# Five units in the opening in place of three, sums kept in SBUF, softmax and last convolution group one pair sooner

## What is computed

```python
c_act = jax.nn.silu(c)
for i in range(DEPTH):                       # DEPTH = 2
    mod = c_act @ ada_w[i] + ada_b[i]        # 2048 x 12288
    sh_mix, sc_mix, g_mix, sh_mlp, sc_mlp, g_mlp = jnp.split(mod, N_MOD, axis=-1)
    h = modulate(rmsnorm(x, norm_mix[i]), sh_mix, sc_mix)   # h*(1+scale)+shift
    mix = fox_mixer(h, ...) if i % 2 == 0 else short_conv_mixer(h, ...)
    x = x + g_mix[:, None, :] * mix
    h = modulate(rmsnorm(x, norm_mlp[i]), sh_mlp, sc_mlp)
    x = x + g_mlp[:, None, :] * (square(relu(h @ mlp_w_up[i])) @ mlp_w_down[i])
return rmsnorm(x, final_norm)
# fox_mixer: q, k, v, f_logit = split(h @ w_in); log_f = log_sigmoid(f_logit + b_f)
#   p = softmax(q k / sqrt(128) + F_t - F_s, causal), F = cumsum(log_f); (p @ v) @ w_out
# short_conv_mixer: b, c, u = split(h @ w_in); (b * conv3(c * u)) @ w_out
```

## Time and profile before

| | |
|---|---|
| median of the timed runs | 2360.25 us |
| the profiled execution's own time | 2361.78 us |
| its span, first to last instruction | 2360.1 us |
| PE (tensor) busy | 2299.3 us, 97% |
| DVE (vector) busy | 1629.4 us, 69% |
| ACT (scalar) busy | 1051.3 us, 45% |
| chain that ended last | PE 90%, DMA 4%, DVE 3%, ACT 2% |
| mean granted tensor clock | 0.987 |
| read from HBM | 611.62 MB, 260 GB/s over the span |

### The profile page before, as it was taken

How to read it: one execution, slowest core, us unless ns; L and a number is a source line. 1 busy time by engine, 2 the same in 40 slices (tenths; PEclk the granted TensorE clock), 3 DMA queues, 4 the chain that set the end, 5 groups by cost and what they waited for, 6 DMA issues and landing times.

```text
span 2360.1 us, 29049 instructions
## 1 busy us (share of the span) xinstructions
PE 2299.3 (97%) x11331; PEld 1941.2 (82%) x11331; DVE 1629.4 (69%) x1539; ACT 1051.3 (45%) x1183; POOL 172.7 (7%) x339
## 2 busy tenths in 40 slices
PE   6999999989999999999998999999999999999998
PEld 6899998878888888888887888877888888888886
DVE  5758989767867866866867887756785455455455
ACT  4344444355434434434445444445543543543443
POOL 0001111101101100100100111100110000000000
PEclk8999999999999999999999999999999999999999
DMA  9978999859968968978976889854995555555563
GB/s 363 387 262 298 336 323 349 295 174 305 334 222 275 327 234 274 322 240 274 314 264 201 317 307 342 297 177 147 310 326 192 183 193 190 188 188 191 191 200 121
DMA packets 270530, 615.61 MB, mean 261 GB/s; under 512 B 14704, under 2 KB 15040, under 8 KB 269504
## 3 DMA queue, kind: packets, MB, share of 16 engines
q1 hardware_dynamic: 220480, 437.29, 54.3%
q0 software_dynamic: 46080, 167.79, 20.1%
q10 hardware_dynamic: 3840, 8.68, 1.1%
HBM read 611.62 MB, written 2.10 MB: 260 GB/s over the span
## 4 chain that ended last, share of the span: by engine, by line
PE 90%; DMA 4%; DVE 3%; ACT 2%; issue 1%; SPq 0%; ACTq 0%; DVEq 0%
PE ps L442 26%; PE ps L444 26%; PE ps L443 26%; DMA start_ring<-in_ada_w_dram 4%; PE ps L429 2%; PE ps L431 2%; PE ps L430 2%; PE ps L721 1%; PE ps L482 1%; PE ps L479 1%; ACT w_hi L791 1%; DVE acc L1198 1%; DVE w_lo L1183 0%; ACT scratch L951 0%; SPq L348 0%
## 5 line engine op out<-in xcount | busy, mean ns | idle before, releaser
L1183 DVE TENSOR_TENSOR w_lo<-raw,w_hi 128x1024 fp32r<-128x1024 f32 x740 | 902.8, 1223 | 590.3 <-ACT w_hi L791 588.3
L791 ACT ACTIVATE w_hi<-raw 128x1024 fp32r<-128x1024 f32 x740 | 783.5, 1060 | 1123.9 <-PE ps L444 1039.6
L442 PE MATMUL ps<-w_hi,h 128*128 128x512 f32 x1536 | 607.5, 396 | 6.5 <-DVE h L1298 6.5
L444 PE MATMUL ps<-w_lo,h 128*128 128x512 f32 x1536 | 600.9, 391 | 0.0
L443 PE MATMUL ps<-w_hi,h 128*128 128x512 f32 x1536 | 600.3, 391 | 0.0
L442 PE MATMUL ps<-w_hi,mid 128*128 128x512 f32 x1280 | 503.9, 394 | 2.6 <-DVE mid L1696 2.6
L444 PE MATMUL ps<-w_lo,mid 128*128 128x512 f32 x1280 | 499.4, 390 | 0.0
L443 PE MATMUL ps<-w_hi,mid 128*128 128x512 f32 x1280 | 499.4, 390 | 0.0
L442 PEld LDWEIGHTS ps<-w_hi,h 128*128 128x128 f32 x1536 | 290.0, 189 | 68.7 <-issue 9.3
L444 PEld LDWEIGHTS ps<-w_lo,h 128*128 128x128 f32 x1536 | 289.8, 189 | 61.5
L443 PEld LDWEIGHTS ps<-w_hi,h 128*128 128x128 f32 x1536 | 290.2, 189 | 58.6 <-issue 0.5
(11 more groups left out here) (202 smaller groups left out, 1235.2 us busy)
## 6 DMA issues: line engine op xcount, KB each, us to landing
ada_raw<-in_ada_w_dram POOLq DMA_DIRECT2D x320, 512.0 KB, 6.4
raw<-in_mlp_w_up_dram SPq DMA_DIRECT2D x128, 1024.0 KB, 5.3
raw<-in_mlp_w_down_dram SPq DMA_DIRECT2D x128, 1024.0 KB, 6.2
raw<-in_fox_w_in_dram SPq DMA_DIRECT2D x48, 1024.0 KB, 9.2
raw<-in_conv_w_in_dram SPq DMA_DIRECT2D x48, 1024.0 KB, 7.6
start_ring<-in_ada_w_dram SPq DMA_DIRECT2D x64, 512.0 KB, 11.7
raw<-in_fox_w_out_dram SPq DMA_DIRECT2D x16, 1024.0 KB, 8.2
raw<-in_conv_w_out_dram SPq DMA_DIRECT2D x16, 1024.0 KB, 5.3
```

The costliest lines, as they stand in the source:

```text
L442: mm(o, xh, hi, start=(k == 0), stop=False)
L444: last = mm(o, xh, lo, start=False, stop=(k == KC - 1))
L791: op(w_hi[:, e % WR], raw[:, e // 2, EK * (e % 2):EK * (e % 2 + 1)], ACT.Copy).then_inc(hi_ready, 1)
L1183: v.tensor_tensor(w_lo[:, e % WR], raw[:, e // 2, EK * (e % 2):EK * (e % 2 + 1)], w_hi[:, e % WR].bitcast(F32), ALU.subtract).then_inc(spl ...
```

## The change

- **Opening.** Five units are opened: k0, v0, q0, k1, q1 (units 1, 2, 0, 4, 3), ten pairs for each m. k0 and q0 accumulate in their own banks as before. v0, k1 and q1 (`SHARED`) share banks 4 and 5 in turns: each multiplies its two pairs of m; then the scalar engine copies (m = 0) or the vector engine adds (`add_part`, later m) the banks to a part in SBUF, and the next tenant starts. Parts lie in xnT's first blocks and in `scratch`. In the queue of the tensor engine the first two pairs of a round now stand ahead of its first tile. SP has five quarters for each m between the tiles in place of three. The closing roundings take the parts (`round_part`, `low_part`). Heads of group 1 are kept in `mid`, those of group 0 in `qs`, `ks`.
- **Attention.** Group 0 now runs in units 5 and 6, group 1 in 6 and 7, groups 2 and 3 as before at units 8 and 11; `maxima`, `exps` and `normalise` stand one pair earlier.
- **Steps.** Units 5 to 11 have 10, 9, 8, 9, 10, 11, 9 steps (before, units 3 to 11 had 8, 9, 8, 9, 10, 8, 9, 11, 8) and the output units 10, 10, 10, 0 (before 2, 10, 4, 0). Gate tile (2, 1) comes ahead of (4, 1), and their sums move to slots 15 and 25 behind the start of the output units.
- **Convolution.** The last group's turn, filter and rounding stand one or two pairs earlier.

```diff
-ADA = ([(3, 0), (3, 1), (4, 0), (2, 0), (4, 1), (2, 1)]
+ADA = ([(3, 0), (3, 1), (4, 0), (2, 0), (2, 1), (4, 1)]
-ORDER = (1, 0, 2)
+N_START = 5
+ORDER = (1, 2, 0, 4, 3)
+SHARED = (2, 4, 3)
+PAIRS = 2 * N_START
-PLAN_QKV = plan([NONE] * 3 + [DENSE, NINE, DENSE, NINE, TEN, DENSE, NINE, [2, 1, 2, 1, 1, 2, 1, 1], DENSE]
-                + [[0] * 6 + [1, 1], TEN, [1] * 4 + [0] * 4, NONE])
+PLAN_QKV = plan([NONE] * N_START + [TEN, NINE, DENSE, NINE, TEN, ELEVEN, NINE] + [TEN, TEN, TEN, NONE])
...
-        QKV_SUM, QKV_STORE = sums_of(PLAN_QKV, {3: (8 * U_OUT0 + 5, 8 * U_OUT0 + 6), 4: (8 * U_OUT0 + 7, 8 * U_OUT0 + 8),
-                                                 5: (8 * U_OUT0 + 22, 8 * U_OUT0 + 22)})
+        QKV_SUM, QKV_STORE = sums_of(PLAN_QKV, {3: (8 * U_OUT0 + 5, 8 * U_OUT0 + 6), 4: (8 * U_OUT0 + 15, 8 * U_OUT0 + 16),
+                                                 5: (8 * U_OUT0 + 25, 8 * U_OUT0 + 25)})
...
             def start_pair(n):                                   # tensor
                 u, e = start_order(n)
+                first, end = 0, KC
                 if n == 0:
                     pe.wait_ge(x_copied, NG)
+                if u in SHARED:
+                    first, end = NB * (e // 2), NB * (e // 2 + 1)
+                    if e % 2 == 0:
+                        pe.wait_ge(part_done, len(SHARED) * (e // 2) + SHARED.index(u))
                 pe.wait_ge(split_ready, n + 1)
                 pe.wait_ge(h_ready, e + 1)
...
-                start_tile(m, 1)
                 start_pair(n)
                 start_pair(n + 1)
+                start_tile(m, 1)
+                start_pair(n + 2)
+                start_pair(n + 3)
                 start_tile(m, 3)
-                start_pair(n + 2)
+                start_pair(n + 4)
+                start_pair(n + 5)
                 start_tile(m, 5)
                 forget_logits(m - 1)
+                start_pair(n + 6)
+                start_pair(n + 7)
                 start_tile(m, 7)
-                start_pair(n + 3)
                 start_sum(m)
...
+            def first_part(i):                                   # scalar, m = 0
+                act.wait_ge(split_used, shared_end(i))
+                op(parts[i], ps[:, 4:6, :], ACT.Copy).then_inc(part_done, 1)
...
+            def add_part(m, i):                                  # vector, m > 0
+                dve.wait_ge(split_used, PAIRS * m + shared_end(i))
+                dve.wait_ge(part_done, len(SHARED) * m + i)
+                v.tensor_tensor(parts[i], ps[:, 4:6, :], parts[i], ALU.add).then_inc(part_done, 1)
...
                 elif t == 2:                                     # vector hooks of a v unit
-                    extra = {3: lambda: maxima(g), 5: lambda: normalise(g)}
+                    extra = {2: lambda: maxima(g), 4: lambda: normalise(g)}
...
-                             None if n else {1: lambda: turn_conv(2 * NG - 1)})
+                             None if n else {0: lambda: turn_conv(2 * NG - 1)})
...
-                         None if n else {2: lambda: conv_last_tap(NG - 1), 4: lambda: conv_round(NG - 1)})
+                         None if n else {1: lambda: conv_last_tap(NG - 1), 2: lambda: conv_round(NG - 1)})
...
-                extra = None if n else {2: lambda: conv_taps(NG - 1), 4: lambda: conv_low(NG - 1)}
+                extra = None if n else {1: lambda: conv_taps(NG - 1), 2: lambda: conv_low(NG - 1)}
```

More of the change, by code:

```diff
@@ L153, in build @@
         prob1 = flat[:, NB * P:NB * P * 3].rearrange("p (j t) -> p j t", j=NB)
-        f_half, f_z, f_e, f_log = [flat[0:H, T * i:T * (i + 1)] for i in range(4)]
+        f_half, f_z, f_e, f_log = [acc[0:H, T * i:T * (i + 1)] for i in range(4)]
+        parts = [xnT[:, 0:NB, :].rearrange("p j t -> p (j t)").rearrange("p (b n) -> p b n", b=2),
+                 scratch[:, 0, :, :], scratch[:, 1, :, :]]
         start_accs = [a.rearrange("p (b n) -> p b n", b=2) for a in (acc[:, :], square_out[:, :])]
@@ L244, in build @@
         exp_done = sem("exp_done")
+        part_done = sem("part_done")
+        second_ready = sem("second_ready")
         norm_p = sem("norm_p")
@@ L417, in _, with chan_pair @@
             turn = nc.tensor.transpose
-            def chan_pair(un, e, rhs, slot=None):
+            def chan_pair(un, e, rhs, slot=None, first=0, end=KC):
                 slot = e % WR if slot is None else slot
@@ L427, in chan_pair, with tok_pair @@
                         jc = slice(P * j, P * (j + 1))
-                        mm(o, hi[:, jc], xh, start=(k == 0 and j % 2 == 0), stop=False, skip_group_check=True)
+                        mm(o, hi[:, jc], xh, start=(k == first and j % 2 == 0), stop=False, skip_group_check=True)
                         mm(o, hi[:, jc], xl, start=False, stop=False, skip_group_check=True)
-                        last = mm(o, lo[:, jc], xh, start=False, stop=(k == KC - 1), skip_group_check=True)
+                        last = mm(o, lo[:, jc], xh, start=False, stop=(k == end - 1), skip_group_check=True)
                 return last
-            def tok_pair(un, e, lhs, slot=None, blocks=range(TT)):
+            def tok_pair(un, e, lhs, slot=None, first=0, end=KC, blocks=range(TT)):
                 slot = e % WR if slot is None else slot
@@ L441, in tok_pair @@
                         xh, xl = lhs[:, k, 0, P * a:P * (a + 1)], lhs[:, k, 1, P * a:P * (a + 1)]
-                        mm(o, xh, hi, start=(k == 0), stop=False)
+                        mm(o, xh, hi, start=(k == first), stop=False)
                         mm(o, xl, hi, start=False, stop=False)
-                        last = mm(o, xh, lo, start=False, stop=(k == KC - 1))
+                        last = mm(o, xh, lo, start=False, stop=(k == end - 1))
                 return last
@@ L613, in _ @@
             forget_logits(NG - 1)
-            for i in range(6):
+            for i in range(PAIRS):
                 start_pair(n + i)
@@ L984, in _ @@
                 elif t == 2:
-                    after = {4: lambda: exps(g)}
-                body(at(u), {7: lambda: round_qkv(u)}, after)
+                    after = {3: lambda: exps(g)}
+                body(at(u), first, after)
             def square_after(i, r0, n, a):
@@ L1483, in _ @@
                 elif t == 2:
-                    extra = {3: lambda: maxima(g), 5: lambda: normalise(g)}
-                body(at(u), {7: lambda: low_qkv(u)}, stores(QKV_STORE, u, qkv_store, extra), PLAN_QKV[0][u], 0)
+                    extra = {2: lambda: maxima(g), 4: lambda: normalise(g)}
+                body(at(u), first, stores(QKV_STORE, u, qkv_store, extra), PLAN_QKV[0][u], 0)
             def gate_ready(r, n):
@@ L1493, in gate_ready @@
                 if first is not None:
-                    dve.wait_ge(mod_ready, first + n // 2 * (2 if r == R_OUT0 else 1) + 1)
+                    dve.wait_ge(mod_ready, first + n // 2 + 1)
             def add_gated(un, n, r):
```

221 lines of the change are left out of this document (144 added, 77 removed).

## The result

The changed kernel takes 2367.61 us (median of 20 runs, 2361.58 to 2370.93) against 2360.28 us (median of 20, 2359.02 to 2361.84). The ratio of the means is 1.0025 [1.0019, 1.0031]: slower by 0.25%, where 2350.5 had been forecast. The profiled execution of the changed kernel has a span of 2368.9 us, that of the kernel before 2360.1, 8.8 less.

The account below looks back on a forecast made before the run. The tensor engine, busy 97% of the span, was taken as the bound, so only pauses and low-clock matmuls could go. 6.5 + 3.8 + 2.8 - 6.0 + 2.6 = 9.7 us gained gave 2350.5, range 2344 to 2358.

Parts of the forecast that it names:

- sums 38 to 39 us apart and a granted clock of 1.0 from 60 to 190: Sign of being right in the opening: start sums of the second and third group so spaced, tensor clock never lowered.
- The opening, 6.5 forecast: Opening of the projections: pauses for ada_w tiles and slow matmuls behind them go, 6.5 us gained, bounds 2 and 7.
- the second and third interval gain their pause and their slow part: Opening, between start sums: pauses of 1.95 and 0.77 and 1.7 of low clock behind each go, 6.4 us gained.
- The head's loss: Start of the opening: tensor begins with pair 0, which needs h, at 46.2 instead of a tile at 44.41; 1.8 lost.
- Units 5 to 11, 4.4 forecast: Softmax a pair sooner: all three tensor waits for normalised probabilities go, 4.4 us gained.
- The output units, 3.8 lost forecast: Output units up to the norm: 6.0 lost for the last sum and 0.6 at mix(3), less 2.8 for the gate sum.
- the wait of the last sum: Unit 15, behind pair 1: tensor waits 4.0 us for vector step 96, bounds 1 and 9; 6.0 lost with its slow part.
- mix(3): Start of the output units: last group's low probabilities come late from the vector engine, a new tensor pause of 0.6 us.
- held pair by pair only from a lag of 5.9; the lag peaks near 5.5: Output units: vector engine's lag peaks near 5.5 us at unit 14, so its splits stay ahead of tensor.
- The convolution, 2.6 forecast: Last convolution group: the 2.64 pause and its slow part go, a shorter wait at the turn comes; 2.6 gained, bounds 0 and 3.5.
- (b): Rival: pauses come back elsewhere, last sum waits 8, thin covers in units 6 to 8 fail; 2359, chance 0.13.
- (c): Rival: opening's hand-overs of banks 4 and 5 come late, 25 us lost over eleven; 2376, chance 0.06.

Follow-up runs that it names:

- half the steps: Changed kernel with the last 30 ada steps done by the vector engine over 512 of 1024 columns, all bytes still moved; 2352.88 us.
- half the moves: Changed kernel with the last 30 ada tiles moved at half their columns, the vector engine doing all its steps in full; 2363.54 us.
- three cures: Changed kernel with a pair between last tile and start sum, the last ada sum two pairs later, and unit 5's ten steps reordered; 2349.75 us.

## Why the prediction was wrong

The forecast named its own sign: sums 38 to 39 us apart and a granted clock of 1.0 from 60 to 190. They stood 40.24 apart, with 0.95 from 60 to 200.

**The opening, 6.5 forecast, 1.2 lost.** The step that failed is "the second and third interval gain their pause and their slow part". The other parts of the term held once the clock was cured: 38.7 between sums (38.76), no transfers as the bound, hand-overs of the banks at 0. The head's loss was 1.2 larger in the profiled execution of the changed kernel (pair 0 at 47.60, forecast 46.2), and the other 6.6 of the 7.7 missed are the low clock. The pauses went, the slow part did not, because the change itself made a new cause for it: it moved the pair that stood between the last tile and the start sum. I read low clocks only behind pauses, since the kernel before has none elsewhere from 51 on, and priced the order of the narrow matmuls at nothing. This cause is shown by taking the meeting out of the one kernel and putting it into the other. The Trainium skill ("TensorE: Matmul & The Clock Gate", section What's actually happening) has the gate go by how busy the engine has been, with the lower level as that of an idle one. If the busy time of the profile is what counts, the stretch behind 82.99 would by that have stayed at the upper level, since no idle time stands ahead of it. The trace disagrees with that reading: from 82 to 88 tensor is busy all 6.00 us, the granted clock is 0.72, and it costs 1.7 us.

**Units 5 to 11, 4.4 forecast, nothing gained.** The three pauses for the probabilities went as forecast; alone, in the kernel before, the edit gave 2.7 us for two of them. The failed part is one that I did not look at: the first mix, now in unit 6, came behind steps of a full unit 5. It waits 1.59 at 242.91 (0.16 more from start to start), and behind it the clock falls (0.52 from 244 to 250), which costs 3.1 us more: these units take 199.4 us here and 196.4 in the run with the pair between tile and sum, where the same wait of 1.60 had no slow part behind it. Together 4.8, all of the 4.7 that are missing. Of five profiled kernels with this wait of 1.6 the clock fell in three (the changed one, half the steps, half the moves) and not in two; why stays open. Two steps moved forward in unit 5 took the wait away: no wait at the first mix is left in the run of three cures.

**The output units, 3.8 lost forecast, 10.7 lost.** The mechanism was right and the sizes were off. In the prediction's terms, against the 96.7 us that the old stretch has without its pause and slow part: the wait of the last sum 5.2 (4.0 forecast), its slow part 4.0 (2.0), mix(3) 0.67 (0.6), and 3.7 left over, which I put at 0 ("held pair by pair only from a lag of 5.9; the lag peaks near 5.5"). Sum 13.6. Of the 3.7 the rows name 1.75 as two waits for a split (0.31 at 445.95, 1.44 at 471.52); the rest is not named by a row. The failed step is thus the size of the lag. Step 96 ended at 490.87, 86.6 us after unit 12 began, where I had 81.6; the vector engine's waits for ada_raw in that stretch are 4.6, near the whole difference. I had them as 0.3 to 1.5, added to the last sum's wait alone and not to the lag of the splits. A margin of 0.4 us (5.9 for 5.5) stood against an error of 5, so the spread of the lag wanted working out, and not its middle.

**The convolution, 2.6 forecast, 3.2 gained.** The wait at the turn is 0.82 (0.9 to 1.1 forecast) and has no slow part.

**The rivals.** (b), pauses that come back elsewhere, at 2359 and a chance of 0.13, was the nearest by its mechanism; it had the last sum and a thin cover ahead of it right (the first mix), but nothing of the clock in the opening. By its number (c), 2376, was as near, with a mechanism that did not occur. None of the cases had the clock fall without a pause, so the range ended 10 us short. No part was waited for in the changed kernel; in an experiment one was, once.

## What to carry to other kernels

Where one-column matmuls stand together for 3.5 us, put wide ones between them: here one pair's place was worth 6.6 us in the opening, with not one pause there in the profile. It shows in the time only where the tensor engine is the bound. Before work is moved into a stretch, add up the other engine's load over all of it with its waits for data inside the sum, and ask what stands behind the last item; two further pairs ahead of the waiting sum were worth 7 us. And look for the idle time of an engine where the work could go instead: the last round of the opening took seven steps for nothing, once none of them stood ahead of the add that hands a bank over.
